# Conditioning matrix streamed through the residual's buffer during the mixing, for the next layer too; residual kept in DRAM meanwhile; weight slots shared out anew

## The reference, cut to what matters

```
for each layer l:
    mod = silu(c) @ ada_w[l] + ada_b[l]       # (1024) x (1024, 6144); six vectors of 1024:
                                              # shift1, scale1, gate1, shift2, scale2, gate2
    h   = rms_norm(x) * (1 + scale1) + shift1 # mixer
    a   = sliding-window attention(h)         # q, kv
    b   = mLSTM(h)                            # mqk, mv, mo; four heads, chunks
    m   = sigmoid(h @ ga) * (a @ w_attn_up) + sigmoid(h @ gb) * (b @ w_mlstm_up)
    x  += gate1 * (m @ w_out)
    h2  = rms_norm(x) * (1 + scale2) + shift2 # channel part
    x  += gate2 * (top-2 of 16 experts: (silu(h2 @ w_gate) * (h2 @ w_up)) @ w_down)
```

## Time and profile before

| | before |
|---|---|
| median of 3 runs | 1732.2 us (1727.72 to 1734.7) |
| span of the profiled execution | 1724.8 us |
| its own time, with what lies around the span | not given apart |
| PE busy | 1506.9 us (87%) |
| DVE busy | 563.9 us (33%) |
| ACT, POOL busy | 323.4 us, 121.8 us |
| moved by DMA | 366.59 MB, mean 213 GB/s |
| mean granted clock of TensorE | 0.940 of full speed |

### The profile page before, as it was taken

One profiled execution on the slowest core, in us unless ns is written; L12 is line 12 of the kernel. 1 busy time (PEld: TensorE's weight loads), 2 busy tenths in 40 slices (PEclk: granted clock), 3 DMA queues, 4 the chain that ended last, 5 costly groups with the idle time before them and its releaser, 6 DMA issues.

```text
span 1724.8 us, 18335 instructions
## 1 busy us (share of the span) xinstructions
PE 1506.9 (87%) x5819; PEld 669.3 (39%) x5820; DVE 563.9 (33%) x1459; ACT 323.4 (19%) x809; POOL 121.8 (7%) x157
## 2 busy tenths in 40 slices
PE   4999999999983999987749999999999387999982
PEld 1544444544441333332335444454444132333330
DVE  1346432446333212111134554243642411221213
ACT  3133411200011212111132343111000121221210
POOL 1100000011101000000111000000110100000001
PEclk8999999999996999999769999999999789999996
DMA  9822111055747899999952111113563799997984
GB/s 307 338 97 98 49 49 49 13 206 173 291 142 268 268 375 379 376 388 360 322 180 98 49 49 50 49 49 108 206 224 145 292 314 381 378 354 247 310 303 165
DMA packets 160813, 366.59 MB, mean 213 GB/s; under 512 B 12433, under 2 KB 14705, under 8 KB 160753
## 3 DMA queue, kind: packets, MB, share of 16 engines
q1 hardware_dynamic: 127568, 256.26, 42.2%
q0 software_dynamic: 21664, 83.89, 12.8%
q10 hardware_dynamic: 11520, 25.70, 5.0%
HBM read 334.37 MB, written 31.46 MB: 212 GB/s over the span
## 4 chain that ended last, share of the span: by engine, by line
PE 69%; DMA 11%; SPq 5%; DVE 5%; issue 4%; ACT 2%; POOL 2%; ACTq 0%; DVEq 0%; POOLq 0%; PEldq 0%
PE bank L939 23%; PE bank L1160 14%; PE bank L929 11%; PE bank L1105 6%; PE bank L1172 6%; DMA weight_ring<-in_w_up_dram 6%; DMA regA<-in_w_up_dram 2%; SPq L428 2%; SPq L431 2%; SPq L371 2%; DMA weight_ring<-in_ada_w_dram 1%; PE bank L1152 1%; PE bank L999 1%; POOL expert_rows L558 1%; PE bank L988 1%
## 5 line engine op out<-in xcount | busy, mean ns | idle before, releaser
L939 PE MATMUL bank<-h_features,weight_ring 128*128 128x512 f32 x768 | 342.4, 599 | 3.1 <-ACT regB L674 1.9
L1160 PE MATMUL bank<-weight_ring,merged_features 128*64 128x512 f32 x960 | 227.2, 628 | 35.3 <-DMA weight_ring<-in_w_up_dram 28.2
L939 PEld LDWEIGHTS bank<-h_features,weight_ring 128*128 128x128 f32 x768 | 144.8, 192 | 182.7 <-issue 182.4
L929 PE MATMUL bank<-weight_ring,h_features 128*128 128x512 f32 (+1 forms) x512 | 196.1, 541 | 1.7 <-ACT h_features L628 1.7
L1703 DVE TENSOR_TENSOR merged_features<-bank,merged_features 64x512 f32<-64x512 f32 x44 | 30.5, 693 | 381.8 <-ACT merged_features L809 381.8
L1160 PEld LDWEIGHTS bank<-weight_ring,merged_features 128*64 128x64 f32 x960 | 73.5, 144 | 165.4 <-issue 160.8
L929 PEld LDWEIGHTS bank<-weight_ring,h_features 128*128 128x128 f32 x512 | 96.0, 190 | 97.0 <-issue 91.6
L1160 PE MATMUL bank<-h_features,merged_features 128*64 128x512 f32 x256 | 117.1, 612 | 11.0 <-DMA regA<-in_w_up_dram 10.0
L1160 PE MATMUL bank<-regA,merged_features 128*64 128x512 f32 x256 | 117.5, 614 | 0.0
L1105 PE MATMUL bank<-weight_ring,merged_features 128*128 128x512 f32 x256 | 110.4, 593 | 3.0 <-POOL merged_features L538 3.0
L1172 PE MATMUL bank<-weight_ring,merged_features 128*64 128x512 f32 x480 | 109.6, 598 | 1.6 <-DVE merged_features L1689 1.6
(11 more groups left out here) (304 smaller groups left out, 1376.1 us busy)
## 6 DMA issues: line engine op xcount, KB each, us to landing
weight_ring<-in_ada_w_dram SPq DMA_DIRECT2D x24, 2048.0 KB, 8.7
weight_ring<-in_w_gate_dram SPq DMA_DIRECT2D x22, 2048.0 KB, 21.1
weight_ring<-in_w_down_dram POOLq DMA_DIRECT2D x22, 2048.0 KB, 14.9
weight_ring<-in_w_up_dram SPq DMA_DIRECT2D x22, 2048.0 KB, 20.4
weight_ring<-in_w_in_dram SPq DMA_DIRECT2D x18, 2048.0 KB, 8.9
h_features<-in_w_gate_dram SPq DMA_DIRECT2D x10, 2048.0 KB, 17.4
regA<-in_w_up_dram SPq DMA_DIRECT2D x10, 2048.0 KB, 27.4
regB<-in_w_down_dram POOLq DMA_DIRECT2D x10, 1536.0 KB, 11.5
```

What stands on the lines that cost most here:

```text
L929: ins = te.matmul(bank[:, 0:w], hT[:, k, P * i:P * i + P], wv[:, k, :], start=(k == 0), stop=(k == KD - 1))
L939: ins = te.matmul(bank[:, :], wv[:, k, c0:c0 + P], rhs[:, k, :], start=(k == 0), stop=(k == kn - 1))
L1160: ins = te.matmul(ps[3][64 * part:64 * part + 64, :], xT[:, k, :], w[:, k, :], start=(k == 0), stop=(k == KD - 1))
```

## The change

- The 12 sums that go over ada_w in a layer are now chunks 4 to 11 of this layer and 0 to 3 of the next (`STREAM`; in the last layer, its own again), all on DVE and PE as chunks 4 to 9 were. Seven stand in the ga and ya stretch (`N_YA` = 7: sum j in turn j, its ones group after ya of the next turn), five in the gb and yb stretch (turns 0 to 4, ones groups after yb of the next turn).
- All of them go through one buffer, `xs`: SP issues the load of chunk n when DVE is through with sum n - 1. So x is written to DRAM after the first norm of the layer and read back after the last sum, ahead of the output projection.
- Layer 0's head stays on PE, with slots 0, 1, 2 and hT. The head of layer 1 is gone; `head_mod` there takes the columns from `modn`. Chunks 10 and 11 on PE after wo, their copies and `bcast` are gone.
- Slots: q, kv, mqk0 in 3, 4, 5, loaded at the end of the layer before; gate 0 and up 0 trade slots; down 1 and down 2 trade places (down 1 in regB and the v buffer). Down 0 and 1 are issued after the last yb, down 2 after wo. The small parameters of the next layer are loaded after wo.

```diff
+STREAM = [(0, c) for c in range(HEAD_ADA, 12)] + [(1, c) for c in range(HEAD_ADA)]
+N_YA = 7
     for j in range(8):
         o += [("ga", j), ("ya", j)]
+        if j >= 1:
+            o += [("ada", j - 1)]
...
-        if j - 1 in MID_ADA:
-            o += [("ada", MID_ADA[j - 1])]
+        if 1 <= j <= len(STREAM) - N_YA:
+            o += [("ada", N_YA + j - 1)]
...
+        ada_w8 = as8(xs[:, :, :].rearrange("p i d -> p (i d)"))
+        SLOT = {"q": 3, "kv": 4, "mqk0": 5, "mqk1": 0, "mv": 1, "mo": 2, "ga0": 3, "ga1": 0, "ya": 1, "yb": 2,
+                "gb0": 3, "gb1": 0, "wo0": 4, "wo1": 5}
...
+                def load_ada(n):
+                    ahead, c_ = STREAM[n]
+                    src = cols8(ada_w, DEPTH - 1 if ahead else l, 512 * c_, 512)
+                    if n:
+                        sp.wait_ge(mid_ready, n)
+                    sp.dma_start(ada_w8, src).then_inc(ada_in, 16)
...
+                load("mqk1")
+                load("mv")
+                load("mo")
...
+                wait_reg(sp, head_xn, l * NT + NT)
+                sp.dma_start(xsave.rearrange("(i p) d -> p i d", p=P), xs[:, :, :]).then_inc(x_kept, 16)
+                wait_reg(sp, x_kept, l * 16 + 16)
+                load_ada(0)
...
+                for n in range(1, N_YA + 1):
+                    load_ada(n)
+                    if n == 4:
+                        through(sp, "ga", 3)
+                        load("gb0")
+                through(sp, "ga", 7)
+                load("gb1")
...
+                through(sp, "ya", 7)
                 load_gate(0, 0)
+                through(sp, "hmT", NT - 1)
+                load("wo0")
+                load("wo1")
+                for n in range(N_YA + 1, len(STREAM)):
+                    load_ada(n)
+                    if n == N_YA + 2:
+                        through(sp, "gb", 3)
+                        load_gate(1, 1)
+                sp.wait_ge(mid_ready, len(STREAM))
+                sp.dma_start(xs[:, :, :], xsave.rearrange("(i p) d -> p i d", p=P)).then_inc(x_back, 16)
+                through(sp, "gb", 7)
                 load_up(0, 0)
+                through(sp, "wo", 2 * NT - 1)
                 load_up(1, 1)
+                with sp.If(l < DEPTH - 1):
+                    sp.wait_ge(x_upd, NT)
+                    params(nxt)
...
+                    wait_reg(sp, gu_ready, blocks_through(sp, E - 3))
+                    load_early(nxt, "q")
+                    load_early(nxt, "kv")
+                    wait_reg(sp, y_ready, blocks_through(sp, E - 2))
+                    load_early(nxt, "mqk0")
...
+                def mod_sum(n):
+                    pe.wait_ge(mid_ready, n + 1)
+                    bank = take("ada", n)
+                    if STREAM[n][1] in (4, 5, 10, 11):
+                        ins = te.matmul(bank[:, :], ones[:, :], sum_buf(n), start=True, stop=True)
+                    else:
+                        ins = column_sums(bank, sum_buf(n))
                     ins.then_inc(pj_ready, 1)
...
                     feature_group("ya", j, attn_o, 4, D)
+                    if j >= 1:
+                        mod_sum(j - 1)
...
-                ada_group(G2_ADA)
...
-                ada_group(G2_ADA + 1)
-                bcast(G2_ADA)
-                bcast(G2_ADA + 1)
...
+                def sum_ada(n):
+                    dve.wait_ge(ada_in, 16 * n + 16)
+                    acc = sum_buf(n)
+                    link(ve.tensor_scalar(acc, ada_w8[:, 0, :], cz[:, 0, 0:1], None, ALU.mult))
                     for k in range(1, KD):
+                        link(ve.scalar_tensor_tensor(acc, ada_w8[:, k, :], cz[:, k, 0:1], acc, ALU.mult, ALU.add))
                     ve.sem_inc(mid_ready, 1)
...
+                    if j >= 1:
+                        mod_chunk(j - 1)
+                    if j < N_YA:
+                        sum_ada(j)
...
+                    if 1 <= j <= len(STREAM) - N_YA:
+                        mod_chunk(N_YA + j - 1)
+                    if j < len(STREAM) - N_YA:
+                        sum_ada(N_YA + j)
+                dve.wait_ge(x_back, 16)
```

More of the change, by code:

```diff
@@ L295, in mix_item @@
-            if name == "wo":
-                return lay(w_out, l)[:, 512 * part:512 * part + 512, :].rearrange("a (k p) n -> p (a k) n", p=P), D, 4
-            return cols8({"ya": w_attn_up, "yb": w_mlstm_up}[name], l, 0, D), D, 4
-        def slot(name, part, k, w):
-            return ring[:, ITEMS[ITEM[(name, part)]][2], 0:k * w].rearrange("p (k n) -> p k n", k=k)
-        def before(n):
-            return [it[2] for it in ITEMS[:n]].count(ITEMS[n][2])
+                return slot(name, 8, w), cols8(w_in, l, c0, w)
@@ L1303, in _ @@
                 head_norm(0, i)
-            head_mod(0)
+            head_cols(0)
+            for j in range(HEAD_ADA):
+                dve.wait_ge(head_bc, j + 1)
+                hlink(ve.tensor_copy(modc[:, 4 * j:4 * j + 4], ps[2 + j % 2][:, 0:4]))
+                ve.sem_inc(head_read, 1)
+            head_mod(modc[:, 0:16])
             with dve.Fori(0, DEPTH) as l:
```

263 lines of the change are left out of this document (103 added, 160 removed).

## The result

The changed kernel takes 1812.6 us (median of 4 runs, 1810.19 to 1818.32) against 1730.7 us (4 runs, 1727.72 to 1734.7): ratio 1.0479, 95% interval [1.0457, 1.0501]. It is 81.9 us slower. The sign was forecast, the size was not: 53.8 us, a time of 1786 with a range up to 1806.

What follows compares the result with a forecast made beforehand. PE alone was taken to bound the mixing, PE with some DMA waits the products. Mixing costs of 2 x (15.2 + 17.6) = 65.6 us less 11.8 of gains gave +53.8: 1786 us, range 1755 to 1806.

Steps and rivals of the forecast that it cites:

- the stretch of ga and ya: Mixing: PE waits for ya's bank in three turns, plus ones matmuls, +17.6 us per layer; bound 25.7 with lowered clock.
- rival A: ga turns: each of six new PE waits of 3.3 us lowers the clock, costing 16 us: 1802 us; chance 0.12.
- The stretch of gb and yb: Mixing: one buffer makes load and sum alternate, 14.2 us per chunk against 11.5; +15.2 us per layer.
- nearly through: yb turns: gate 1's load, issued some 6 us ahead of a chunk load, would be almost finished by then.
- The output projection: First output matmul to router: no change, 0 us; removing the two chunks behind it also 0, bounds -1 and +1.
- The experts' term: Expert products: loading down 1 before them gains nothing in layer 0 and 2 us in layer 1, at most 5.5.
- The parameters' -4: Layer 0's expert products: moving the fourteen parameter loads out from between experts 14 and 15 saves 4 us, between 0 and 11.
- The boundary: Between layers: adds no longer held up by head_mod, -4.8 us; gather sooner, -1 us; new loads there delay nothing.
- the first case: Main forecast over the whole kernel: +53.8 us, 1786 us, own range 1762 to 1803; chance 0.69 together with D.
- B: Expert products: every PE wait for weights goes, 38.2 us, with 4.8 at the layer boundary: 1755 us; chance 0.13.
- C: Both mixing stretches: the chunk stream is hidden, only six more ones groups stay: 1734 us, down to 1702; chance 0.06.
- D: Layer boundary doesn't shorten, because the gathers land later: 1791 us; chance counted within the first case's 0.69.

Runs made afterwards that it cites:

- the two retimed kernels: Changed kernel with chunk sums shared out by turn and a second buffer, 1747.0 us; the same plus down 1 and four mixing loads late, 1739.8 us.

## Why the prediction was right in sign and wrong in size

**The step that failed** is the one on the stretch of ga and ya, in its last term. The banks, the three turns, the instruction that releases PE and the wait (3.3 forecast, 3.40 to 3.85 measured) were right. But rival A was put aside because the wait lay "just below" the 3.28 us behind which the trace showed a full clock, and it got a chance of 0.12. All six waits of the profiled execution were followed by a train at the lower clock: (9.85 - 7.1) + (9.70 - 7.1) + (9.94 - 7.1) and the like in layer 1, 16.3 us. With it the stretch is 2 x 17.6 + 16.3 = 51.5 of the 52.5 measured. The run in which PE is kept at work shows the cause: same order, same release, full clock in turns 2 and 6 of both layers. The error was to read two waits as a bound on the length of a wait. The wait of 3.28 us stood behind long dense expert products; these stand in a stretch with small mLSTM matmuls; whether that makes the difference isn't shown. And even here a wait doesn't settle it. Seven traces have the six waits, 3.39 to 3.86 us long, and 40 of the 42 are followed by a train of 8.5 to 10.1 us. Two are followed by one of 7.10, both the first of layer 1; the kernel with down 1 late has one of them, here with the wait that follows it:

```profile
1167.65 7.10 PE L956 MATMUL bank<-h_features,weight_ring 128*128 128x512 f32 x16 [3.40 <-DVE merged_features L1561]
...
1199.37 9.29 PE L956 MATMUL bank<-h_features,weight_ring 128*128 128x512 f32 x16 [3.85 <-DVE merged_features L1561]
```

Such differences between executions of one program fit the spread of 8 us in the runs of the changed kernel and part of the 10 us by which the two profiled ones differ more than the medians; that they make all of it isn't shown. The Trainium skill's page TensorE: Matmul & The Clock Gate, section HAM oscillation — how this bites in real kernels, had warned of a kernel that waits in each turn; the trace agrees, with six trains of 9.7 to 9.9 us for 7.1.

**The stretch of gb and yb:** mechanism and size right, +15.2 forecast, +17.0 and +16.9 measured. The missing 1.8 is the one load behind gate 1, 10.08 us instead of 7.9: "nearly through" was 2.2 us short.

**The output projection** was taken to be untouched, +3.9 us. PE comes to it after a wait for POOL's last add, and I didn't ask what the clock does behind my own 2.3 us of emptying. Luck has a part here: behind the same wait ten of 18 trains were as fast as before.

**The experts' term** has the wrong sign in layer 1: -2 forecast, +5.4 measured, of which putting down 1 back takes 5.8 away (3.6 to 6.6 by the nine traces). I priced the transfer by the bytes that it frees, and didn't ask what DMA could do instead in those 10 us: with no buffer free, the bytes leave a gap. The parameters' -4 is what the edit is worth inside the changed kernel (4.1), but against before layer 0 has only 1.4 of it, and by the same edit alone the kernel before gains 1.2 there.

**The boundary:** the gathers and adds shortened as forecast (16.5 us; 16.1 to 17.0 in all traces of changed kernels, 18.5 to 24.4 in the three of the kernel before and its variants), but last down to first gather and last adds to first q grew, by 3.1 us against the forecast. Of the new loads there, which I took to be hidden since "nothing waited for them", mqk0 has a part: without it ahead the first gather comes 2.9 us sooner. The rest, in DVE's wait at the start of layer 1, stays open.

**Rivals.** A was true, on top of the first case: its 1802 came with the same errors in the small terms. B, C failed: waits for weights rose by 3 us, and nothing of the stream was hidden. D was half true. Put together: 53.8 + 16.3 (clock in ga) + 1.0 (rest of that stretch) + 3.5 (yb) + 3.9 (wo) + 10.0 (experts) + 3.1 (boundary) + 0.3 = 91.9, the difference of the spans; the medians differ by 81.9. The small terms all erred the same way, since each gain was taken as what an edit frees and each new load as hidden.

## What to carry to other kernels

A wait put into a train of matmuls costs its own length and then what the clock takes from the train behind it (here 3.4 us and 2.7 us); two waits in a trace, one with a fall and one without, are no bound, and 0.12 was too little for what then came 40 times in 42. Before a load is moved ahead, look at what DMA would do in its old place: if every buffer is in use there, nothing is gained, and what runs ahead may collide later. In a loop in which engines take turns in order, the turn in which a job lies has a part in its price: seven sums cost 26 us with a ones group in each turn, 15 to 19 with the ones groups kept out of the turns with m_finish, and five sums in turns chosen for them cost 5.3.

## What was not expected of the hardware

- The clock fell behind eight of 18 waits of 2.27 and 2.28 us (ahead of wo), behind all four of 2.83 us (in the two retimed kernels) and behind 40 of 42 of 3.39 to 3.86 us (ahead of ga), while the earlier trace rows show full speed behind 3.28 us. With PE kept at work ahead of it, a wait of 1.27 us was still followed by a train of 8.80 us. The length of the wait alone does not decide.
- Three matmuls whose result nobody reads, 2.6 us of PE in each of six turns, made the kernel 13 us faster.
- A load of 2 MB behind another of 2 MB issued some 6 us earlier took 10.1 us against 7.9 alone. An up load that SP had issued took 42.2 us in the kernel in which POOL issued a down load of 2 MB 6 us sooner, and 34.9 in the other; no run moved that load alone.
- Between the layers DVE stood 12.42 us ahead of its first instruction of layer 1, without a releaser that the profile shows. Over all the kernels it is 9.1 to 12.9 us, and with the same loads as here it is 9.09 in the kernel with the ones groups in pairs.
